# Attention over one blended band of 128 keys, with a step's transposes ahead of the value products of the step in front

## What is computed

```python
s_band = jnp.einsum('bnqkgd,bnskd->bnkgqs', qb, k_band).astype(F32) * scale   # block of 128 queries, 256 keys: block before + own
s_meta = jnp.einsum('bnqkgd,bmkd->bnkgqm', qb, k_meta).astype(F32) * scale    # 16 meta keys, always visible
band_ok = (kpos >= BLOCK) & (diff >= 0) & (diff < WINDOW)                     # WINDOW = 128
probs = softmax(concat([sink, s_meta, s_band]))
o = einsum(p_meta, v_meta) + einsum(p_band, v_band)                           # then o @ w_o + b_o
```

## Time and profile before

| | |
|---|---|
| median of 3 runs | 2263.78 us (2263.52 to 2265.49) |
| profiled execution: time, span | 2260.66 us, 2258.9 us |
| mean granted TensorE clock | 0.933 |
| PE, DVE, ACT, POOL busy | 88%, 71%, 55%, 17% of the span |
| phase_attend in the span | about 1286.6 to 1551 us |

### The profile page before, as it was taken

One profiled execution on the slowest core, in us unless ns is written; L12 is line 12 of the kernel. 1 busy time (PEld: TensorE's weight loads), 2 busy tenths in 40 slices (PEclk: granted clock), 3 DMA queues, 4 the chain that ended last, 5 costly groups with the idle time before them and its releaser, 6 DMA issues. The chain is left out here.

```text
span 2258.9 us, 31492 instructions
## 1 busy us (share of the span) xinstructions
PE 1993.8 (88%) x10714; PEld 1580.3 (70%) x10714; DVE 1606.3 (71%) x1635; ACT 1252.4 (55%) x1457; POOL 375.5 (17%) x683
## 2 busy tenths in 40 slices
PE   4769999669999999997299899998499999999991
PEld 3558777458888888886287656666388888888880
DVE  8995221558888888886722277773588888888885
ACT  6524110447777777775301155554277777777772
POOL 1000000311122211221211111012012221111214
PEclk9979999779999999999599879999799999999995
DMA  3355100649999999995421110004299999999985
GB/s 98 43 53 187 49 0 1 246 147 367 379 375 366 370 372 374 382 378 225 147 58 47 38 57 1 1 1 166 107 341 356 364 372 385 382 379 390 382 319 233
DMA packets 134859, 504.66 MB, mean 223 GB/s; under 512 B 38322, under 2 KB 68338, under 8 KB 83570
## 3 DMA queue, kind: packets, MB, share of 16 engines
q1 hardware_dynamic: 115074, 468.83, 57.1%
q0 software_dynamic: 18432, 33.86, 4.0%
q10 hardware_dynamic: 1280, 0.98, 0.3%
HBM read 488.47 MB, written 47.32 MB: 237 GB/s over the span
## 5 line engine op out<-in xcount | busy, mean ns | idle before, releaser
L1406 DVE TENSOR_TENSOR moe_lo<-moe_raw,moe_hi 128x2048 fp32r<-128x2048 f32 x378 | 860.7, 2291 | 120.4 <-ACT moe_hi L1191 119.3
L1191 ACT CAST moe_hi<-moe_raw 128x2048 fp32r<-128x2048 f32 x374 | 714.2, 1914 | 155.0 <-PE moe_ps_g L1546 76.3
L1544 PE MATMUL moe_ps_g<-moe_hi,moe_x_hi 128*128 128x512 f32 x512 | 212.3, 415 | 7.8 <-DVE moe_x_lo L1411 4.7
L1544 PE MATMUL moe_ps_y<-moe_hi,moe_h_hi 128*128 128x512 f32 x512 | 208.6, 407 | 3.7 <-DVE moe_h_lo L1422 3.7
L1545 PE MATMUL moe_ps_g<-moe_hi,moe_x_lo 128*128 128x512 f32 x512 | 206.5, 403 | 0.0
L1546 PE MATMUL moe_ps_g<-moe_lo,moe_x_hi 128*128 128x512 f32 x512 | 206.1, 403 | 0.0
L1545 PE MATMUL moe_ps_y<-moe_hi,moe_h_lo 128*128 128x512 f32 x512 | 203.5, 398 | 0.0
L1546 PE MATMUL moe_ps_y<-moe_lo,moe_h_hi 128*128 128x512 f32 x512 | 203.1, 397 | 0.0
L1546 PE MATMUL moe_ps_u<-moe_lo,moe_x_hi 128*128 128x512 f32 x512 | 203.0, 396 | 0.0
L1544 PE MATMUL moe_ps_u<-moe_hi,moe_x_hi 128*128 128x512 f32 x512 | 202.8, 396 | 0.0
L1545 PE MATMUL moe_ps_u<-moe_hi,moe_x_lo 128*128 128x512 f32 x512 | 202.8, 396 | 0.0
(11 more groups left out here) (399 smaller groups left out, 3745.8 us busy)
## 6 DMA issues: line engine op xcount, KB each, us to landing
moe_raw<-moe_w_gate SPq DMA_DIRECT2D x128, 1024.0 KB, 6.8
moe_raw<-moe_w_up SPq DMA_DIRECT2D x128, 1024.0 KB, 7.8
moe_raw<-moe_w_down SPq DMA_DIRECT2D x128, 1024.0 KB, 7.2
moe_raw<-y_dram SPq DMA_DIRECT2D x16, 1024.0 KB, 11.6
mix_r<-ssm_w_glu SPq DMA_DIRECT2D x16, 512.0 KB, 5.7
xn_dram<-moe_work SPq DMA_DIRECT2D x16, 512.0 KB, 7.2
mix_r<-x SPq DMA_DIRECT2D x8, 512.0 KB, 5.2
mix_r<-h_dram SPq DMA_DIRECT2D x16, 256.0 KB, 11.5
```

Of the source, the lines that this page charges most:

```text
L1191: A.copy(hi[:, slot(number, k), :], raw[:, k, :]).then_inc(hi_done, 1)
L1406: V.tensor_tensor(lo[:, slot, :], raw[:, k, :], hi[:, slot, :].bitcast(F32), ALU.subtract).then_inc(lo_done, 1)
L1544: T.matmul(out, x_h, w_h, start=first, stop=False)
```

## The change

- Scores, blocks 1 to 7: instead of one masked add, ACT copies the scores of the block in front into `sm` (`copy_prev`, 2 x 128 wide), DVE overwrites them with the own scores where a 0/1 mask says so (`copy_predicated`, 2 x 128) and copies the 2 x 16 meta scores. In block 0 DVE adds a mask over 2 x 128 and copies the meta scores. `sm` and `pr` hold 145 columns per head.
- Maximum, exponentials and multiplications run over 145, 145 and 144 columns per head in all blocks (the multiplications take in 16 meta columns and 128 of the band).
- Transposes: three instead of six (four in block 0): one per head, 128 wide, and one for the 32 meta columns of both heads. `ps_t` and `pt` are doubled by step, so the transposes wait for the copy of two steps before.
- ACT copies 256 wide and 32 partitions x 128.
- DVE `keep_own`: the transposed weights times a triangular 0/1 mask, 2 x 128 (`p_own`), blocks 1 to 7. Once per block a difference of value blocks, 256 wide (`v_step`).
- Value products: a pair with the values of the block in front and all weights, one product with `v_meta` (32 rows deep, 128 columns: a block diagonal of both heads), a pair with `v_step` and `p_own`. In block 0 a pair and the `v_meta` product.
- `v_meta` is zeroed by POOL and filled by two small DMAs that SP issues ahead of the loads of `w_o`.
- PE order: `transpose_weights(s)` ahead of `outputs(s - 1)`.

```diff
         @block.sync
+            sp.wait_ge(zeros_set, 1)
+            for r in range(H2):
+                sp.dma_start(v_meta[r * N_META:(r + 1) * N_META, :, r * DH:(r + 1) * DH],
+                             v_sb[0:N_META, XT, :].rearrange("p (k d) -> p k d", d=DH)).then_inc(v_meta_in, 16)
...
         @block.scalar
+            def copy_prev(s):
+                prev = key_run(s // DC)[2]
+                act.wait_ge(sc_mm, s + 1)
+                if s >= 2:
+                    act.wait_ge(exp_done, 2 * (s - 1))
+                A.copy(window(sm, s), banks(s)[:, :, prev:prev + P]).then_inc(prev_set, 1)
...
-                w = 2 * P if s >= DC else P
-                A.copy(pt[:, s % 2, :, 0:w], ps_t[:, :, 0:w])
-                A.copy(pt[0:N_META, s % 2, :, 2 * P:], ps_t[0:N_META, :, 2 * P:3 * P]).then_inc(pt_done, 1)
+                A.copy(pt[:, s % 2, 0:2 * P], ps_t[:, s % 2, 0:2 * P]).then_inc(wt_set, 1)
+                A.copy(pt[0:2 * N_META, s % 2, 2 * P:], ps_t[0:2 * N_META, s % 2, 2 * P:3 * P]).then_inc(pt_done, 1)
...
             for s in range(NS):
+                if DC <= s + 1 < NS:
+                    copy_prev(s + 1)
                 exps(s)
...
         @block.vector
-                V.tensor_tensor(sm[:, s % 2, :, 1:1 + w], ps_s[:, 2 * (s % 2):2 * (s % 2) + 2, 0:w],
-                                visible.unsqueeze(1).to_broadcast([P, H2, w]), ALU.add).then_inc(sm_done, 1)
...
+                    dve.wait_ge(prev_set, s - DC + 1)
+                    V.copy_predicated(window(sm, s), is_own[:].bitcast(U32).unsqueeze(1).to_broadcast([P, H2, P]),
+                                      own_scores).then_inc(score_step, 1)
+                V.tensor_copy(meta_part(sm, s).rearrange("p (r m) -> p r m", r=H2),
+                              banks(s)[:, :, meta:meta + N_META]).then_inc(sm_done, 1)
...
+            def keep_own(s):
+                dve.wait_ge(wt_set, s + 1)
+                if s >= DC + 2:
+                    dve.wait_ge(pv_mm, s - 1)
+                V.tensor_tensor(p_own[:, s % 2, :].rearrange("p (r m) -> p r m", r=H2),
+                                pt[:, s % 2, 0:2 * P].rearrange("p (r m) -> p r m", r=H2),
+                                own_t[:].unsqueeze(1).to_broadcast([P, H2, P]), ALU.mult).then_inc(own_set, 1)
...
                 normalize(s)
+                if s - 1 >= DC:
+                    keep_own(s - 1)
                 if s >= 2:
                     o_lo_part(s - 2)
+                if c == 5 and i + 1 < XT:
+                    if i:
+                        dve.wait_ge(pv_mm, DC * i)
+                    V.tensor_tensor(v_step[:, (i + 1) % 2, :], v_sb[:, i + 1, :], v_sb[:, i, :], ALU.subtract).then_inc(v_step_set, 1)
...
         @block.tensor
                 pe.wait_ge(norm_done, H2 * (s + 1))
-                if s:
-                    pe.wait_ge(pt_done, s)
+                if s >= 2:
+                    pe.wait_ge(pt_done, s - 1)
                 for r in range(H2):
...
+                    T.transpose(ps_t[:, s % 2, r * P:(r + 1) * P], window(pr, s)[:, r, :], ident[:])
+                T.transpose(ps_t[0:2 * N_META, s % 2, 2 * P:3 * P], meta_part(pr, s), ident[:]).then_inc(pt_mm, 1)
...
                 for r in range(H2):
-                    T.matmul(outs[r], v_sb[:, i, vc], w[r][:, 0:P], start=True, stop=False)
+                    T.matmul(outs[r], v_sb[:, max(i - 1, 0), vc], pt[:, s % 2, r * P:(r + 1) * P], start=True, stop=False)
+                last = T.matmul(ps_o[:, 0:P], v_meta[:, c // 2, :], pt[0:2 * N_META, s % 2, 2 * P:], start=False, stop=(i == 0))
                 if i:
+                    pe.wait_ge(own_set, s - DC + 1)
+                    pe.wait_ge(v_step_set, i)
                     for r in range(H2):
-                        T.matmul(outs[r], v_sb[:, i - 1, vc], w[r][:, P:2 * P], start=False, stop=False)
-                for r in range(H2):
-                    last = T.matmul(outs[r], v_sb[0:N_META, XT, vc], w[r][0:N_META, 2 * P:], start=False, stop=True)
+                        last = T.matmul(outs[r], v_step[:, i % 2, vc], p_own[:, s % 2, r * P:(r + 1) * P], start=False, stop=True)
                 last.then_inc(pv_mm, 1)
...
                 if s + 2 < NS:
                     scores(s + 2)
+                transpose_weights(s)
                 if s >= 1:
                     outputs(s - 1)
-                transpose_weights(s)
```

More of the change, by code:

```diff
@@ L1871, in phase_attend @@
         wo_hi, wo_lo = (sb(f"wo_{x}", [P, DC, D], F32R) for x in ("hi", "lo"))
-        sm = sb("sm", [P, 2, H2, 1 + SC_W])
+        sm = sb("sm", [P, 2, 2 * HEAD + 2 * N_META])
         nm = sb("nm", [P, 2, H2])
-        pr = sb("pr", [P, 2, H2, 1 + SC_W])
+        pr = sb("pr", [P, 2, 2 * HEAD + 2 * N_META])
         rs = sb("rs", [P, 2, H2])
         rinv = sb("rinv", [P, 2, H2])
-        pt = sb("pt", [P, 2, H2, 3 * P])
+        pt = sb("pt", [P, 2, 3 * P])
+        p_own = sb("p_own", [P, 2, H2 * P])
+        v_step = sb("v_step", [P, 2, KV])
+        v_meta = sb("v_meta", [2 * N_META, N_KV, P])
         o_hi, o_lo = (sb(f"o_{x}", [P, 2, DC, P], F32R) for x in ("hi", "lo"))
         ps_s = ps("ps_s", [P, 4, 512])
-        ps_t = ps("ps_t", [P, H2, 512])
+        ps_t = ps("ps_t", [P, 2, 512])
         ps_o = ps("ps_o", [P, 512])
@@ L1887, in phase_attend @@
                              "w_lo_done"))
+        zeros_set, v_meta_in, prev_set, score_step, wt_set, own_set, v_step_set = (
+            sem(x) for x in ("zeros_set", "v_meta_in", "prev_set", "score_step", "wt_set", "own_set", "v_step_set"))
         sc_mm, sm_done, nm_done, exp_done, rinv_done, norm_done, pt_mm, pt_done, pv_mm, o_hi_done, o_lo_done, y_mm, h_done = (
@@ L1894, in width, with banks, window, meta_part @@
             return SC_W if s >= DC else N_META + P
[L1896 to L1901, removed]
+        def banks(s):
+            return ps_s[:, 2 * (s % 2):2 * (s % 2) + 2, :]
+        def window(x, s):
+            return x[:, s % 2, 1:1 + 2 * (P + 2 * N_META)].rearrange("p (r m) -> p r m", r=H2)[:, :, 0:P]
+        def meta_part(x, s):
+            return x[:, s % 2, 1 + P:1 + P + 2 * N_META]
+        def head(x, s, r):
+            return x[:, s % 2, r * HEAD:(r + 1) * HEAD]
         def y_bank(i, half):
@@ L1924, in _ @@
             G_ = nc.gpsimd
[L1925 to L1933, removed]
+            G_.memset(v_meta[:], 0.0).then_inc(zeros_set, 1)
+            G_.memset(own_only[:], 0.0).then_inc(mask_step, 1)
+            G_.memset(is_own[:], 1.0).then_inc(mask_step, 1)
+            G_.memset(own_t[:], 1.0).then_inc(mask_step, 1)
+            pool.wait_ge(mask_step, 3)
+            for own, fill, sign in ((own_only, NEG, 1), (is_own, 0.0, 1), (own_t, 0.0, -1)):
+                G_.affine_select(out=own[:], in_=own[:], compare_op=ALU.is_ge, fill=fill, base=0, pattern=[[-sign, P]],
+                                 channel_multiplier=sign).then_inc(mask_step, 1)
             pool.wait_ge(small_in, 16)
@@ L1953, in exps @@
                 for r in range(2):
-                    A.activation(pr[:, s % 2, r, 0:1 + width(s)], sm[:, s % 2, r, 0:1 + width(s)], ACT.Exp,
-                                 bias=nm[:, s % 2, r:r + 1],
+                    A.activation(head(pr, s, r), head(sm, s, r), ACT.Exp, bias=nm[:, s % 2, r:r + 1],
                                  accum_out=rs[:, s % 2, r:r + 1]).then_inc(exp_done, 1)
@@ L1990, in scores @@
             def scores(s):
+                own, prev, meta = key_run(s // DC)[1:]
                 dve.wait_ge(sc_mm, s + 1)
@@ L1994, in scores @@
                     dve.wait_ge(exp_done, 2 * (s - 1))
[L1995 to L1998 removed]
+                own_scores = banks(s)[:, :, own:own + P]
+                if s < DC:
+                    V.tensor_tensor(window(sm, s), own_scores, own_only[:].unsqueeze(1).to_broadcast([P, H2, P]),
+                                    ALU.add).then_inc(score_step, 1)
+                else:
+                    dve.wait_ge(prev_set, s - DC + 1)
[3 more added lines that the diff above has]
+                              banks(s)[:, :, meta:meta + N_META]).then_inc(sm_done, 1)
+                dve.wait_ge(score_step, s + 1)
                 dve.wait_ge(sm_done, s + 1)
                 dve.wait_ge(sink_set, s + 1)
[L2001 removed]
+                V.reduce_max(nm[:, s % 2, :], sm[:, s % 2, 0:2 * HEAD].rearrange("p (r m) -> p r m", r=H2), AX.X,
+                             negate=True).then_inc(nm_done, 1)
             def normalize(s):
@@ L2040, in _ @@
                     add_projection(i - 2, 1)
+            keep_own(NS - 1)
             o_lo_part(NS - 2)
```

24 lines of the change are left out of this document (8 added, 16 removed).

## The result

The changed kernel takes 2267.86 us, median of 12 runs (2264.35 to 2270.17), beside 2263.86 for the kernel before, also of 12 (2261.39 to 2265.49). The ratio is 1.0017, 95% interval 1.0009 to 1.0025: slower by 0.2%, where 2245.8 us was forecast and the range ended at 2256.

What follows compares the result with a forecast made beforehand. PE was taken to bound blocks 1 to 7. Transposes -18.2, value products +2.8, block 0 -3.3, step 8 -0.6 and the start +1.3 sum to -18.0: 2263.8 becomes 2245.8 us, range 2236 to 2256.

Steps and rivals of the forecast that it cites:

- PE bounds blocks 1 to 7, DVE and ACT are in time in an ordinary step.: Blocks 1 to 7: DVE 3.11 and ACT 2.37 us lie below the new 3.54 us step, slack 1.0 and 0.7.
- Rival 1: DVE and ACT hold PE up in the attention steps; half way 2253.5 us, range 2250 to 2262; chance 0.10.
- Three transposes less, 3 x 0.11 per step.: Blocks 1 to 7: six transposes become three, 0.33 us off each of 55 steps, 18.2 us off.
- There are as many changes of depth per step, four.: Value products, blocks 1 to 7: depth changes stay four per step, so most of the gap pattern stays as before.
- +2.8: Value products, blocks 1 to 7: 0.05 us more in each of 55 steps, ends -5.5 and +8.3.
- Rival 2: Value product slots: one switch more at four places, 0.32 us per step; only block 0 gains, 2261 us; chance 0.04.
- The addition to h [...] eat the slack for a step each.: Blocks 1 to 7: the addition to h, twice a block, and v_step, once, use up the slack; no cost given.
- Block 0, -3.3: Block 0: steps of about 3.1 us for 3.65, six times 0.55, 3.3 us off, ends 1.5 and 4.5.
- the start, +1.3: Start: v_meta's DMAs wait for POOL ahead of the w_o loads on SP's queue, 1.3 us more, ends 0.6 and 2.0.
- step 8 (-0.6): Step 8, first with six transposes and still at half clock: three fewer at 0.21 us, 0.6 us off.
- rival 3: From step 9 on: PE idling lowers the granted clock, 20 us per block lost, 2286 us with two; chance 0.04.
- 1.40 us for 896 columns: DVE, slowest two-source form in the trace: scaled to 0.44 us for 256 columns, beside the 0.42 used.

Runs made afterwards that it cites:

- e5: Kernel before, with the 16 row meta products made 128 rows deep by zero rows: 2253.21 us, ratio 0.9956.
- e6: Changed kernel with the old PE order and the meta product as a pair of 64 columns, padded to 128 rows: 2243.3 us, ratio 0.9917.
- e4: Changed kernel with the meta product behind both pairs and the old PE order: 2256.54 us, ratio 0.9973.
- e2: Kernel before with only the new PE order, transposes ahead of the value products of the step in front: 2270.85 us, ratio 1.0037.
- e1: Changed kernel with the old PE order, value products ahead of the transposes: 2263.51 us, ratio 1.0004.
- e3: Changed kernel in its own order, with the meta product moved behind both pairs: 2260.57 us, ratio 0.9988.
- e12: Changed kernel with the single meta product 128 rows by 128 columns, moved ahead of the pairs, right behind the transposes: 2248.41 us, ratio 0.9933.
- e11: Changed kernel with the single meta product made 128 rows by 128 columns, left between the pairs: 2267.85 us, ratio 1.0022.
- e10: Changed kernel with v_meta's two DMAs behind the first two loads of w_o on SP's queue: 2267.09 us, ratio 1.0016.

## Why the prediction was wrong, point by point

- **PE bounds blocks 1 to 7, DVE and ACT are in time in an ordinary step.** Right. copy_predicated took 0.45 for the 0.42 taken, keep_own 0.41 for 0.42, the meta copy 0.18 for at most 0.26. Rival 1, DVE and ACT holding PE up in most steps, did not come.
- **Three transposes less, 3 x 0.11 per step.** The records did go; the three that stay took 0.47, not the 0.38 forecast, as they have a change behind them now. With the order and the change of shape kept, three transposes are worth what was forecast: e5 to e6, 3.67 to 3.34.
- **The step that failed: "There are as many changes of depth per step, four."** It counted depth, so that 128 by 64 pairs and 128 by 128 transposes passed for one kind, and it did not ask who the transposes' new neighbours are. By the shape of the stationary tile there were four and are six. The value products were given +0.05 per step; what the edit costs beside the transposes is 0.05 for the wide product (e4), 0.19 for the order (e2, and e1 against after), 0.15 for the meta product between the pairs (e3): 0.39. So +2.8 should have been about +21, against -18.2. e3 and e5 each take away one change and moved the step by 0.15, e2 adds one with the order and moved it by 0.19, and e12 takes away two against e11 and moved it by 0.35.
- The trace of before had it. In the earlier trace rows the first transpose stands 0.16 in front of the second and 0.37 behind the last value product's start, and the prediction read both, the one as a property of first transposes, the other as one of depth.
- **Rival 2, the product slots take it back,** was the right mechanism with the wrong count: four places with 0.08 each, 0.32, where it is two more places of 0.15 and 0.04 from the order. It was given 0.04 because "there are no more changes than before", the same miscount.
- **"The addition to h [...] eat the slack for a step each."** It named DVE's own addition, not POOL's, and priced nothing. POOL's addition cost 0.49 in one step of each block, 2.9 us in all. The slack had been counted at 1.0 us (it is 1.6 in the longer step that came out); the hold is 1.87, and PE idles 0.27, to which come 0.07 and 0.15 at the next starts.
- **Block 0, -3.3, and the start, +1.3.** With step 8 (-0.6) they were to gain 2.6 and gained 1.0. Steps 2 to 7 gained 3.1 of the 3.3, step 8 0.4 of the 0.6. The start is what was mis-sized: the first split came 1.2 later, as forecast, but the first steps lost 2.5. The rest is the order, which the forecast had as a gain alone: in the changed kernel PE stands 2.62 us at the transposes of step 1, and the value products of step 0, which went first before, stand behind them. e2, which has the order alone, takes 12.52 for 11.10 there, e1, which has the new loads and the old order, 11.52.
- **The clock, rival 3,** stayed at 1.00 from step 9 on. But the reading behind the rival, 0.50 where PE idled 14%, does not hold up as a reason: the earlier trace rows has 0.50 also with PE busy 6.62 of 6.70 us, and the kernel after has it with 10.49 of 10.90.
- A slip without weight: 1.40 us for 896 columns makes 0.40 for 256 if all of it scaled, not 0.44; the 0.42 taken was that of another row.

Set into the forecast of -18.0, the products' and the order's 18.6 more, the 2.9 of the holds and the 1.6 missing up to step 9 make +5.1, where the phase grew by 5.3 and the medians lie 4.0 apart.

## What to carry to other kernels

Count the changes of the stationary tile's shape in PE's order (rows and columns both, narrow transposes with the wide ones), before and after an edit, and look for loads that start with their product, not ahead of it: small products sort by shape, and a shallow one is better padded with zeros to its neighbour's shape, or placed beside its like. Moving a group of instructions changes both its old and its new neighbours, also where nothing about the group changes. When the bound engine waits for another once a block, look at what a third engine runs then: here cutting POOL's addition into four brought 9 us, half of what the change itself was meant to bring. The new band with the old order, padded meta products and the cut addition (e8) makes 2233.62 us, 1.4% below the kernel before.

## What the runs showed of the hardware that was not expected

**A change of tile shape on PE costs about 0.15 us at full clock.** The product behind it starts 0.09 to 0.10 later than within a shape, its second record another 0.05 (0.10 at the wide meta product). Which shape changes into which made no difference beyond that in the shapes tried, with 16, 32, 64 and 128 rows and 64 and 128 columns. Transposes of 16 or 32 columns were the exception: no change between them and the 128 wide ones or the projection. The Trainium skill ("TensorE: Matmul & The Clock Gate", Part 3, The mechanism) says in its list of what overlaps that a weight load overlaps with running products only when its row group differs from theirs, while the text above the list also has loads pulled ahead into a background weight buffer. The trace disagrees with the list: between two projection products of the same 128 rows the load of 1403.22 runs while the product of 1403.12 (0.51 long) does. Here it is a different shape at which loads stop running ahead. That the late load is the whole cause of the gap is not shown; from 1340 to 1500 us the two come together at every place in all 14 traces (0.00 ahead in the median at a change, 0.03 to 0.23 within a shape). The 0.04 that the new order costs beside its change has a place but no cause: in the old order the projection starts 0.03 behind the last transpose, less than the 0.11 between transposes, and its second record 0.32 behind its first; in the new order the pair stands 0.20 behind the last transpose, and the projection's second record 0.34 behind its first.

**POOL's addition of two SBUF tensors stops DVE's multiplication by a scalar.** 0.50 became 2.37 in after and e6 and 0.73 in e8, and in all three the multiplications ended 0.30 behind POOL's instruction. In the kernel before the same addition stretched them from 0.63 to 1.37, and nobody waited. The Trainium skill ("SBUF — State Buffer", Who interferes with whom) has the two engines share one port pair, which goes to whoever starts first for its whole instruction, and names tensor_scalar among the instructions that can take it when their operands allow a two-port mode. The trace agrees: POOL was first each time (0.31 us ahead in after, e6 and e8), and DVE's two short instructions took 2.37 us in after and e6. At the start of e10 DVE was first, by 0.30 (1294.14 and 1294.44), and its multiplications took their usual 0.50, POOL's addition 2.41. No run here looks at the ports themselves.
